# A hybrid decoder step on one core: GpSimd's subtractions wait for the order of the experts, the branch register is loaded ahead of the last pass, and the sums are copied out in halves

## The reference

```python
scores = jax.nn.sigmoid((x @ router_w).astype(jnp.float32))
sel = scores + router_b
grp_score = jnp.sum(lax.top_k(sel.reshape(T, N_GROUPS, -1), 2)[0], axis=-1)
_, gidx = lax.top_k(grp_score, TOPK_GROUPS)          # 4 of 8 groups
...
_, eidx = lax.top_k(jnp.where(emask, sel, -jnp.inf), TOP_K)
w = jnp.take_along_axis(scores, eidx, axis=1)
w = w / jnp.sum(w, axis=-1, keepdims=True) * ROUTED_SCALE
routed = routed_experts(x, eidx, w, wg, wu, wd)      # sum of w * ((silu(x wg) * (x wu)) wd)
shared = (jax.nn.silu(x @ swg) * (x @ swu)) @ swd
x = x + g2 * (routed + shared)
```

## Time and profile before

| what | value |
|---|---|
| time of three runs | 1621.33, 1622.3, 1633.79 us; median 1622.3 |
| profiled execution | 1629.76 us, span 1628.0 us |
| mean granted TensorE clock in it | 0.954 |
| busy: PE, DVE, ACT, POOL | 93%, 25%, 21%, 3% of the span |
| chain that ended last | PE 82%, DMA 8%, ACT 3%, DVE 3%, issue 2% |

### The profile page before, as it was taken

The page is one execution under the profiler, slowest core; times in us unless marked ns, Lnnn a source line. Parts: engine busy times, 40 slices in busy tenths (PEclk is TensorE's granted clock), DMA queues, the critical chain, the costliest instruction groups (busy, mean ns, idle before and its releaser), DMA issues.

```text
span 1628.0 us, 21788 instructions
## 1 busy us (share of the span) xinstructions
PE 1510.0 (93%) x8868; PEld 804.4 (49%) x8868; DVE 414.3 (25%) x996; ACT 345.4 (21%) x921; POOL 49.2 (3%) x86
## 2 busy tenths in 40 slices
PE   5997997999999999999899989799999999999995
PEld 2444664545455445454355445454444545445543
DVE  1116515212212112221153233421111211122113
ACT  2114413111111111111253222401111111111112
POOL 0000201000000000000010010100000000000000
PEclk7998989999999999999989998999999999999996
DMA  9867423899999989999952252188999998999981
GB/s 394 344 262 310 165 75 122 359 384 365 421 421 415 378 340 421 422 413 374 376 218 103 104 192 82 56 359 316 352 422 420 418 372 343 423 421 407 377 342 33
DMA packets 65892, 509.64 MB, mean 313 GB/s; under 512 B 7776, under 2 KB 8048, under 8 KB 10208
## 3 DMA queue, kind: packets, MB, share of 16 engines
q1 hardware_dynamic: 62064, 490.17, 74.5%
q0 software_dynamic: 3728, 18.07, 3.0%
HBM read 499.16 MB, written 11.01 MB: 313 GB/s over the span
## 4 chain that ended last, share of the span: by engine, by line
PE 82%; DMA 8%; ACT 3%; DVE 3%; issue 2%; SPq 1%; ACTq 0%; DVEq 0%
PE bank L1765 24%; PE banks L1793 11%; PE banks L1709 8%; DMA s_gu_ring<-in_moe_wu_dram 8%; PE banks L421 5%; PE banks L1018 3%; PE ybank L1730 3%; PE banks L641 3%; PE bank L1733 3%; PE banks L1730 3%; PE bank L475 2%; PE banks L1046 2%; PE banks L1555 1%; PE bank L1718 1%; PE bank L487 1%
## 5 line engine op out<-in xcount | busy, mean ns | idle before, releaser
L1765 PE MATMUL bank<-s_gu_ring,s_hbuf 128*32 128x512 f32 (+1 forms) x2560 | 420.0, 610 | 26.0 <-DMA s_gu_ring<-in_moe_wu_dram 24.3
L1765 PEld LDWEIGHTS bank<-s_gu_ring,s_hbuf 128*32 128x32 f32 (+1 forms) x2560 | 134.1, 125 | 302.7 <-issue 302.7
L1793 PE MATMUL banks<-s_dn_ring,s_hTs 128*32 128x512 f32 (+1 forms) x1280 | 211.6, 597 | 2.0 <-ACT s_wsl L1819 2.0
L1709 PEld LDWEIGHTS banks<-s_sel,s_htok 128*128 128x128 f32 x1200 | 146.2, 191 | 48.2 <-issue 48.2
L1891 DVE TENSOR_TENSOR s_ylo<-banks,s_yhi 128x512 fp32r<-128x512 f32 x116 | 80.3, 692 | 322.4 <-ACT s_yhi L1839 322.4
L1709 PE MATMUL banks<-s_sel,s_htok 128*128 128x256 f32 (+1 forms) x1200 | 158.1, 287 | 0.5 <-issue 0.5
L1839 ACT CAST s_yhi<-banks 128x512 fp32r<-128x512 f32 x116 | 68.0, 586 | 296.3 <-PE banks L1793 296.3
L1883 DVE SCALAR_TENSOR_TENSOR s_hh<-s_sg,s_wsl,bank 128x256 f32<-128x256 f32 x58 | 27.9, 481 | 388.8 <-ACT s_sg L1829 388.8
L1793 PEld LDWEIGHTS banks<-s_dn_ring,s_hTs 128*32 128x32 f32 (+1 forms) x1280 | 58.8, 122 | 123.1 <-issue 120.9
L1829 ACT ACTIVATE s_sg<-bank 128x256 f32<-128x256 f32 x58 | 22.3, 385 | 404.3 <-PE bank L1765 404.3
L1018 PE MATMUL banks<-s_gu_ring,s_hbuf 128*128 128x512 f32 x128 | 55.9, 593 | 0.5 <-DVE s_rs L1302 0.5
(11 more groups left out here) (410 smaller groups left out, 1541.8 us busy)
## 6 DMA issues: line engine op xcount, KB each, us to landing
s_gu_ring<-in_moe_wg_dram SPq DMA_DIRECT2D x128, 1024.0 KB, 10.2
s_gu_ring<-in_moe_wu_dram SPq DMA_DIRECT2D x128, 1024.0 KB, 12.2
s_dn_ring<-in_moe_wd_dram SPq DMA_DIRECT2D x128, 1024.0 KB, 11.8
s_gu_ring<-in_ada_w_dram SPq DMA_DIRECT2D x24, 2048.0 KB, 9.5
s_gu_ring<-in_win_dram SPq DMA_DIRECT2D x6, 2048.0 KB, 12.4
s_gu_ring<-in_wqkv_dram SPq DMA_DIRECT2D x3, 2048.0 KB, 16.4
s_gu_ring<-in_wo_dram SPq DMA_DIRECT2D x2, 2048.0 KB, 7.7
s_gu_ring<-in_shared_up_dram SPq DMA_DIRECT2D x2, 2048.0 KB, 11.9
```

The costliest lines, as they stand in the source:

```text
L1709: last = pe.matmul(b[:, 256 * (m % 2):256 * (m % 2) + width], w[:, m * P:(m + 1) * P], sel[q % 2][:, s, 0:width], start=(n == 0), stop=(n ...
L1765: last = pe.matmul(W0[o:o + n, :], xg4[:, p % 3, k, o:o + n], w[:, k, :, :], start=(k == 0), stop=(k == KC - 1))
L1793: last = pe.matmul((W1, W2)[half][o:o + n, :], hTs[:, f, o:o + n], dn_ring[:, dn_of[(l, r)][0], w0:w0 + 512], start=(f == 0), stop=(f == 1))
```

## The change

It does three things in `moe` and `rest`. POOL waits for `order_full` ahead of its three subtractions. The register load of `any_left` moves from behind the last pass to ahead of it, on all three engines; its wait is now for the layer's first `gt_full`, and the branches stay where they were. The copy of the sums is reordered and cut: ACT copies the halves of bank 6 first, then the first bank of `ybank` (`acc_out`), then the second (`acc_out2`); DVE copies its pair as two instructions. PE waits for `acc_out2` at its fifth group of transposes. Besides, an increment of a semaphore that nobody waits for (`qprod_full`) is gone.

```diff
@@ -1275,7 +1275,7 @@
                     k2 = qk[:, 4:8, 0:SEQ].rearrange("p h (n t) -> p h n t", n=2)
                     dve.tensor_tensor(qe, qe, qk[:, 0:4, 0:SEQ], ALU.mult)
                     dve.tensor_tensor(qoff, qoff, q2[:, :, :, 64:P], ALU.mult)
-                    dve.tensor_tensor(qi[:, :, :], eb[:, :, :], qk[:, 0:4, :], ALU.mult).then_inc(G["qprod_full"], 1)
+                    dve.tensor_tensor(qi[:, :, :], eb[:, :, :], qk[:, 0:4, :], ALU.mult)
 
                     def ke_mult(u):
                         h, n = order_u[u]
@@ -1412,7 +1412,7 @@
         SEMS = ("r_psum", "r_sig", "tok_psum", "tok_hi", "tok_lo", "sh_psum", "sh_silu", "sh_h", "topk_full",
                 "cnt_psum", "pw_full", "pw_psum", "pwT_full", "perm_full", "sort_psum", "order_full", "h_kept",
                 "sel_full", "fill_full", "fill_act", "fill_dve", "gu_full", "silu_full", "hh_full", "tr_full", "hT_full",
-                "gt_full", "y_full", "y_high", "y_low", "acc_full", "acc_out", "back_psum")
+                "gt_full", "y_full", "y_high", "y_low", "acc_full", "acc_out", "acc_out2", "back_psum")
         S = {n: sem(n) for n in SEMS}
         order = sb("order", [P, NE], I32)
         excess = sb("excess", [P, 2], I32)
@@ -1505,6 +1505,7 @@
                     def _(pool):
                         normed(pool, 2 * l + 1)
                         pool.dma_start(h_saved, hbuf[:, 0:KC * T]).then_inc(S["h_kept"], 16)
+                        pool.wait_ge(S["order_full"], l + 1)
                         for t, (t0, tn) in enumerate(TILES):
                             pool.wait_ge(S["tok_hi"], 6 * l + 2 * t + 2)
                             if t == 2:
@@ -1694,7 +1695,7 @@
                 hTs = sb("hTs", [P, 2, P], c=c2)
                 wsl = [sb(f"wsl{i}", [P, 2], c=c2) for i in range(2)]
                 dg = sb("dg", [P, T], c=c2)
-                rest_pe, rest_act, rest_dve = rest(l, dn_ring, wovS, dg, ovh)
+                any_left, rest_pe, rest_act, rest_dve = rest(l, dn_ring, wovS, dg, ovh)
                 xg4 = hbuf[:, :].rearrange("p (b k s) -> p b k s", b=3, s=P)
                 shown = [(htok[:, 0, 0, :], 0), (htok[:, 0, 1, :], 0), (htok[:, 1, 0, :], 1), (htok[:, 1, 1, :], 1), (htok2[:, :], 2)]
 
@@ -1751,6 +1752,8 @@
                     slot_weights(0).then_inc(S["tr_full"], 1)
 
                     for p in range(NP):
+                        if p == NP - 1:
+                            left = any_left(pe)
                         groups, q = column_groups(PASSES[p]), p // 2
                         ranks = [r for r, _ in PASSES[p]]
                         pe.wait_ge(S["fill_act"], 2 * (l * NQ + q + 1))
@@ -1794,7 +1797,7 @@
                                                      dn_ring[:, dn_of[(l, r)][0], w0:w0 + 512], start=(f == 0), stop=(f == 1))
                             last.then_inc(S["y_full"], 1)
                     pe.wait_ge(S["y_low"], 2 * (l + 1) * NP)
-                    rest_pe(pe)
+                    rest_pe(pe, left)
                     combine(NP - 1).then_inc(S["acc_full"], 1)
 
                 @block.scalar
@@ -1825,6 +1828,8 @@
                     act.wait_ge(S["tr_full"], l * (NP + 1) + 1)
                     slot_out(0).then_inc(S["hT_full"], 1)
                     for p in range(NP):
+                        if p == NP - 1:
+                            left = any_left(act)
                         act.wait_ge(S["gu_full"], l * NP + p + 1)
                         act.activation(sg[:, :], W0[:, 0:FF], ACT.Silu).then_inc(S["silu_full"], 1)
                         if p // 2 + 1 < NQ:
@@ -1838,7 +1843,7 @@
                             act.wait_ge(S["y_full"], 2 * (l * NP + p) + half + 1)
                             act.copy(yhi[:, half, :], (W1, W2)[half]).then_inc(S["y_high"], 1)
                     act.wait_ge(S["y_low"], 2 * (l + 1) * NP)
-                    rest_act(act)
+                    rest_act(act, left)
 
                 @block.vector
                 def _(dve):
@@ -1878,6 +1883,8 @@
                     fill_out(0, 1)
                     fill_out(0, 3)
                     for p in range(NP):
+                        if p == NP - 1:
+                            left = any_left(dve)
                         dve.wait_ge(S["silu_full"], l * NP + p + 1)
                         dve.wait_ge(S["hT_full"], l * (NP + 1) + p + 1)
                         dve.scalar_tensor_tensor(hh[:, :], sg[:, :], wsl[p % 2][:, 0:1], W0[:, FF:2 * FF], ALU.mult, ALU.mult).then_inc(S["hh_full"], 1)
@@ -1889,21 +1896,23 @@
                         for half in range(2):
                             dve.wait_ge(S["y_high"], 2 * (l * NP + p) + half + 1)
                             dve.tensor_tensor(ylo[:, half, :], (W1, W2)[half], yhi[:, half, :].bitcast(F32), ALU.subtract).then_inc(S["y_low"], 1)
-                    rest_dve(dve)
+                    rest_dve(dve, left)
 
                 acct = hbuf[:, :].rearrange("p (t d) -> p t d", d=D)
 
                 @block.scalar
                 def _(act):
                     act.wait_ge(S["acc_full"], l + 1)
-                    act.copy(acct[:, 0, :], ybank[:, :, :].rearrange("p a b -> p (a b)"))
                     act.copy(acct[0:NS, 2, 0:512], bank[6][0:NS, :])
-                    act.copy(acct[0:NS, 2, 512:1024], bank[6][NS:P, :]).then_inc(S["acc_out"], 1)
+                    act.copy(acct[0:NS, 2, 512:1024], bank[6][NS:P, :])
+                    act.copy(acct[:, 0, 0:512], ybank[:, 0, :]).then_inc(S["acc_out"], 1)
+                    act.copy(acct[:, 0, 512:1024], ybank[:, 1, :]).then_inc(S["acc_out2"], 1)
 
                 @block.vector
                 def _(dve):
                     dve.wait_ge(S["acc_full"], l + 1)
-                    dve.tensor_copy(acct[:, 1, :], pair[1][:, :, :].rearrange("p a b -> p (a b)")).then_inc(S["acc_out"], 1)
+                    dve.tensor_copy(acct[:, 1, 0:512], pair[1][:, 0, :]).then_inc(S["acc_out"], 1)
+                    dve.tensor_copy(acct[:, 1, 512:1024], pair[1][:, 1, :]).then_inc(S["acc_out2"], 1)
 
                 c2.close()
                 gate, i = mod[l][:, 40:48, :], 2 * (l + 1)
@@ -1915,6 +1924,8 @@
 
         def back(pe, l, i, acct, b, m, lag):
 
+            if m == KC // 2:
+                pe.wait_ge(S["acc_out2"], 2 * (l + 1))
             if m >= lag:
                 pe.wait_ge(N["x_full"], KC * (i - 1) + m - lag + 1)
             for t, (t0, tn) in enumerate(TILES):
@@ -2052,12 +2063,12 @@
             h_back = sem(f"rest_hT{l}")
 
             def any_left(eng):
-                eng.wait_ge(S["gt_full"], (l + 1) * NP)
+                eng.wait_ge(S["gt_full"], l * NP + 1)
                 return eng.value_load(excess[0:1, 0:1], min_val=0, max_val=T) > 0
 
-            def rest_act(act):
+            def rest_act(act, left):
                 act.wait_ge(S["y_full"], 2 * (l + 1) * NP)
-                with act.If(any_left(act)):
+                with act.If(left):
                     act.dma_start(hbuf[:, 0:KC * T], h_saved).then_inc(h_back, 16)
                     with act.Fori(0, NE) as it:
                         e = act.value_load(order[0:1, bass.ds(it, 1)], min_val=0, max_val=NE - 1)
@@ -2069,8 +2080,8 @@
                             act.activation(ovh[:, f, :], W1[:, 0:T], ACT.Silu).then_inc(silu_in, 1)
                         act.wait_ge(sums_in, it + 1)
 
-            def rest_dve(dve):
-                with dve.If(any_left(dve)):
+            def rest_dve(dve, left):
+                with dve.If(left):
                     with dve.Fori(0, NE) as it:
                         for t, (t0, tn) in enumerate(TILES):
                             last = dve.tensor_scalar(dg[0:tn, t0:t0 + tn], ident[0:tn, 0:tn], wovS[0:tn, t, bass.ds(it, 1)], None, ALU.mult)
@@ -2083,8 +2094,8 @@
                             dve.tensor_tensor(ovh[:, f, :], ovh[:, f, :], W0[:, 0:T], ALU.mult).then_inc(h_in, 1)
                         dve.wait_ge(sums_in, it + 1)
 
-            def rest_pe(pe):
-                with pe.If(any_left(pe)):
+            def rest_pe(pe, left):
+                with pe.If(left):
                     pe.wait_ge(h_back, 16)
                     with pe.Fori(0, NE) as it:
                         pe.wait_ge(dg_in, it + 1)
@@ -2108,7 +2119,7 @@
                                                      start=False, stop=False)
                         last.then_inc(sums_in, 1)
 
-            return rest_pe, rest_act, rest_dve
+            return any_left, rest_pe, rest_act, rest_dve
 
 
         qkv_slots, qkv_in, win_slots, win_in = [], [], {}, {}
```

More of the change, by code:

```diff
@@ L940, in gla @@
                     "zeroed", "a1_psum", "a1_full", "gate_psum", "gate_full", "neg_full", "exp_full", "ln_full", "scan_step", "b_full",
-                    "diff_full", "qk_psum", "qk_full", "decay_full", "qprod_full", "ke_exp", "ke_full", "r_psum", "r_full",
+                    "diff_full", "qk_psum", "qk_full", "decay_full", "ke_exp", "ke_full", "r_psum", "r_full",
```

## The result

The changed kernel takes 1613.14 us in the median of 22 runs (1604.58 to 1621.85), the kernel before, measured beside it, 1623.7 us (22 runs, 1615.47 to 1635.71). The ratio is 0.9934, 95% interval 0.9913 to 0.9955: by the ratio 10.7 us less, between 7.3 and 14.1. The prediction was 1608, range 1602 to 1618. Its sign, its range and three of its four terms held. The fourth, the clock, did not: the number came out where the rival "clock falls anyway" had put it (1612.7).

A forecast was written before the change was run, and what follows sets the result against it. The prediction took PE, with 82% of the chain of waits, to bound the kernel. Holds 7.5, load 1.4, copies 0.7 and clock 4.5 sum to 14.1 us; from the median 1622.3 that gives 1608.2, forecast 1608, range 1602 to 1618.

The forecast's parts named there:

- the clock: Routing: PE resumes after 1.6 us of idling, not 5.3, so its clock stays up; 4.5 us, or 0 if it falls.
- clock falls anyway: Rival, chance 0.25: PE's clock in the routing falls despite the shorter idling; time 1612.7 us.
- Holds: Routing masks: VectorE operations no longer held by GpSimd's subtractions; 7.5 us over two layers, bound 0 if another cause.
- The subtractions' new place: Behind the order: subtractions hold VectorE's L1666 (L1667 after the change) about 2.3 us; cost zero, bound 0 to 1.4 us.
- The load: Ahead of each layer's last scatter: register load leaves PE's gap; 0.80 us in layer 0, 0.62 in layer 1.
- Copies: Copy of the sums: PE waits for two 64-row copies and one half; 0.35 us saved a layer, 0.7 in all.
- The sum: Whole kernel: 7.5 + 1.4 + 0.7 + 4.5 = 14.1 us off the median of 1622.3, forecast 1608.

The follow-up runs named there:

- the copy: Changed kernel plus GpSimd copies, reading one SBUF tensor and writing another, where the subtractions once stood; single time, 1608.51 or 1610.92 us (text doesn't say which).
- the memset: Changed kernel plus write-only GpSimd memsets where the first subtractions once stood; single time, 1608.51 or 1610.92 us (text doesn't say which).
- the one without the wait: Changed kernel without GpSimd's wait for the order, early register load and halved copies kept: 1622.01 us (12 runs), ratio 0.9976 to the kernel before.
- the kernel with a busy tail: Changed kernel plus thrown-away matmuls around each layer's last scatter, two ahead and two behind: 1604.62 us (6 runs), ratio 0.9873 to the kernel before.
- the run with two thrown-away matmuls: Changed kernel plus two 448-column matmuls, results unused, while PE waits for the masks in the routing: 1610.19 us (4 runs), ratio 0.9880 to the kernel before.

## Why the prediction was right, and where it was not

- **Holds (predicted 7.5 us, bound 0).** Right: 7.42 in the gaps, and shown to be GpSimd's reads by the copy and the memset. The matching ends in the earlier trace rows had been the right evidence.
- **The subtractions' new place (predicted 0).** Right. L1667 was held for one subtraction, 2.40 us in all, and PE's transposes at 277.90 had no wait.
- **The load (predicted 0.8 and 0.6).** Right: 0.86 and 0.66. At its new place it costs nothing, as predicted, though it runs beside the matmuls ahead of the wait for weights and not in the wait. With the branch time that the Trainium skill gives (Advanced Engine Details and Errata, Control Flow Timing), an estimated 0.30 us would have been left in the gap (0.57 - 0.27); 0.57 are there.
- **Copies (predicted 0.35 a layer).** Right: 0.31. The second halves never showed in the chain.
- **The clock (predicted 4.5).** Wrong. The step that failed: with PE at work again after 1.6 us of idling, ahead of the point where the clock used to fall, the clock was to stay up. It fell in both layers, about 1 us after PE had taken up work. In layer 0 nothing was won (2.40 and 8.00 us against 2.43 and 7.73). In layer 1 the profiled execution won 1.84, since before the change its low stretch lay so that the 28 took 9.56 us. The low stretch was shorter in the changed kernel's profile (about 3.5 us in each layer, from 6.8 and 10.3) but fell on matmuls all the same. Not all of that is the change's. From the first token copy to the first pass, the twelve places with the short idling take 44.9 to 45.0 us in ten and 46.6 in two; the four places with the hold (the kernel before and the one without the wait) take 48.7 to 50.5. The means differ by 4.3 us a layer, of which 3.7 are the gap. So the clock gave about 1.2 us over both layers instead of 4.5. The price of the fall was not the error: keeping the clock up is worth another 1.60 us a layer. The fallacy was to take the length of the idling as the measure. The waits for weights in the changed kernel's passes contradict it: 3.30 us of idling were followed by a group at full clock (7.07 us), and 2.31 us by a slow one (8.78 us). The row in the prediction's own hands, 0.81 behind 2.12 us, only showed that short idling can bring the clock down, not that shorter is safer.
- **The sum.** Without the clock term the prediction is its own rival: 1622.3 - 9.6 = 1612.7, measured 1613.14 (by the ratio, 0.9934 x 1622.3 = 1611.6). The range held because it had been drawn to take in that rival, which had a chance of 0.25; the forecast of 1608 itself is 5.1 us too low. The time alone would not have shown the error, since the interval of the gain just reaches the 14.1 us that were forecast. The windows showed it. The clock term was the largest guess of the four, and the only one with no row of a matching kind behind it.

The two groups behind those waits, in PE's timeline, and the 28 matmuls of the routing in one of the two long places, layer 0 of the kernel with a busy tail:

```profile
559.13 7.07 PE L1768 MATMUL bank<-s_gu_ring,s_hbuf 128*32 128x512 f32 x64 [3.30 <-DMA s_gu_ring<-in_moe_wu_dram]
...
1375.91 8.78 PE L1768 MATMUL bank<-s_gu_ring,s_hbuf 128*64 128x512 f32 x32 [2.31 <-DMA s_gu_ring<-in_moe_wu_dram]
```
```profile
262.41 9.63 PE banks L1556 x28
```

The measured 10.7 us hold the 9.56 us of the three terms and perhaps about 1.2 of the clock in the routing; the interval can't separate 9.6 from 10.8. That the two profiled executions differ by 16.8 us comes from slow groups in the passes and would have misled anyone who compared only these two.

## What to carry to other kernels

When a small VectorE instruction is many times too long, put its end beside the ends of GpSimd's; if they match, move the GpSimd work behind the point that others wait for, and name the next VectorE instruction that it will hold. When the chain shows PE at the low clock behind a short wait, put work there, real work from later if there is any: in the routing that was worth 6.4 us by the stages, where the change's three parts gave 9.6. Price a clock change only by an execution in which the clock did what the argument needs, else leave it as a range.

## What the runs showed of the hardware that was not expected

- A GpSimd instruction with one SBUF operand holds VectorE as well as one with two; a memset of the same tile doesn't. Even a 128x24 addition and a comparison wait to its end (0.72 us for 0.20, 0.90 for 0.18).
- Work that has been taken up again does not hold the clock: it fell 1 us into full work (1.00, 0.99, 0.50 in the windows of the changed kernel). Only work inside the idling kept it up, as the run with two thrown-away matmuls shows (1.00, 1.00).
- The spread of single executions is mostly the clock: over the 22 runs of the changed kernel (spans 1602.5 to 1619.8 us, mean granted clock 0.969 to 0.956) the span grows by 10.8 us for each 0.01 of clock lost, correlation -0.93. Which of the stalls are followed by a slow group differs from execution to execution; what decides it stays open. Stages that no edit touches differ as well: layer 0's first token copy starts at 252.0 and 252.2 us in the profiles of the memset and the tail kernel and at 259.7 in the changed kernel's, and from 20 to 40 us the granted clock was 0.91 in those two and 0.53 in this one. So a single time, or the difference of two, tells nothing of an effect of a few us.
